# First-head silu written with exponentials, and two steps of the last head moved, in a gated recurrence

## What is computed

```python
q, f, i, g = jnp.split(h @ w_in, 4, axis=-1)
forget = lb + (1.0 - lb) * jax.nn.sigmoid(f)
key_in = 1.0 - forget
log_f = jnp.log(forget)
o = _chunk_gated_recurrence(heads(jax.nn.silu(q)), heads(key_in), heads(i), heads(log_f))
o = _rmsnorm(o, out_norm) * jax.nn.silu(heads(g))
return o.reshape(B, S, D_MODEL) @ w_out
```

## Time and profile before

| | |
|---|---|
| median of 3 runs | 2028.6 us (2027.17 to 2029.3) |
| profiled execution | 2026.63 us |
| its span in the trace | 2024.8 us |
| PE busy | 1992.9 us, 98% |
| DVE, ACT, POOL busy | 47%, 46%, 42% |
| chain that ended last | PE 93%, DVE 4%, ACT 2% |
| recurrence in the trace | about 810 to 1080 us |

### The profile page before, as it was taken

How to read it: one execution, slowest core, us unless ns; L and a number is a source line. 1 busy time by engine, 2 the same in 40 slices (tenths; PEclk the granted TensorE clock), 3 DMA queues, 4 the chain that set the end, 5 groups by cost and what they waited for, 6 DMA issues and landing times.

```text
span 2024.8 us, 26338 instructions
## 1 busy us (share of the span) xinstructions
PE 1992.9 (98%) x10823; PEld 1613.2 (80%) x10823; DVE 953.5 (47%) x1470; ACT 927.1 (46%) x1290; POOL 859.0 (42%) x672
## 2 busy tenths in 40 slices
PE   8999999999999999899999999999999999999999
PEld 7788888878888887677777888888877678888887
DVE  6644443264302316888984553255145545522551
ACT  6666563343313325666564543244366545432441
POOL 2344334526444453343334545444441254444443
PEclk9999999999999999999999999999999999999999
DMA  6122222223322321121112232222210222232321
GB/s 258 52 94 74 73 73 94 100 67 105 103 94 94 104 94 58 69 74 64 64 64 94 94 104 95 94 101 97 78 49 25 79 94 94 94 104 86 102 99 68
DMA packets 51816, 178.30 MB, mean 88 GB/s; under 512 B 5744, under 2 KB 8944, under 8 KB 51568
## 3 DMA queue, kind: packets, MB, share of 16 engines
q1 hardware_dynamic: 51696, 176.61, 25.7%
HBM read 174.49 MB, written 2.10 MB: 87 GB/s over the span
## 4 chain that ended last, share of the span: by engine, by line
PE 93%; DVE 4%; ACT 2%; issue 1%; POOL 1%; DMA 0%; SPq 0%; DVEq 0%; ACTq 0%; POOLq 0%
PE ps_gemm L228 24%; PE ps_gemm L230 24%; PE ps_gemm L229 24%; PE ps_attend L228 4%; PE ps_attend L230 4%; PE ps_attend L229 4%; PE ps_attend L1738 1%; PE ps_attend L890 1%; PE ps_attend L2522 1%; PE ps_attend L2588 1%; PE ps_attend L2523 1%; PE ps_attend L285 1%; PE ps_gemm L1718 0%; PE ps_attend L1767 0%; PE ps_attend L903 0%
## 5 line engine op out<-in xcount | busy, mean ns | idle before, releaser
L2789 POOL TENSOR_TENSOR weights_low<-weights_raw,weights_high 128x512 fp32r<-128x512 f32 (+1 forms) x332 | 427.7, 1288 | 1120.8 <-ACT weights_high L203 1120.6
L228 PE MATMUL ps_gemm<-normed_high,weights_high 128*128 128x512 f32 x1665 | 662.4, 398 | 5.4 <-DVE normed_low L1300 4.7
L230 PE MATMUL ps_gemm<-normed_low,weights_high 128*128 128x512 f32 x1665 | 648.2, 389 | 0.0
L229 PE MATMUL ps_gemm<-normed_high,weights_low 128*128 128x512 f32 x1665 | 647.8, 389 | 0.0
L203 ACT ACTIVATE weights_high<-weights_raw 128x1024 fp32r<-128x1024 f32 (+1 forms) x340 | 339.7, 1006 | 448.5 <-PE ps_attend L230 216.0
L2790 POOL TENSOR_TENSOR weights_low<-weights_raw,weights_high 128x512 fp32r<-128x512 f32 (+1 forms) x332 | 441.6, 1330 | 0.0
L228 PEld LDWEIGHTS ps_gemm<-normed_high,weights_high 128*128 128x128 f32 x1665 | 313.6, 188 | 77.7 <-issue 5.3
L230 PEld LDWEIGHTS ps_gemm<-normed_low,weights_high 128*128 128x128 f32 x1665 | 313.7, 188 | 65.8
L229 PEld LDWEIGHTS ps_gemm<-normed_high,weights_low 128*128 128x128 f32 x1665 | 313.9, 188 | 64.6 <-issue 3.6
L228 PE MATMUL ps_gemm<-operands_high_low,weights_high 128*128 128x512 f32 (+1 forms) x552 | 216.2, 392 | 0.9 <-POOL weights_low L2790 0.5
L230 PE MATMUL ps_gemm<-operands_high_low,weights_high 128*128 128x512 f32 (+1 forms) x552 | 214.2, 388 | 0.0
(11 more groups left out here) (322 smaller groups left out, 2097.7 us busy)
## 6 DMA issues: line engine op xcount, KB each, us to landing
weights_raw<-weights_full SPq DMA_DIRECT2D x317, 512.0 KB, 3.2
weights_raw<-weights_short SPq DMA_DIRECT2D x24, 128.0 KB, 2.0
residual<-x_tiles SPq DMA_DIRECT2D x4, 512.0 KB, 8.5
out_tiles<-residual SPq DMA_DIRECT2D x8, 256.0 KB, 2.1
parameters<-params SPq DMA_DIRECT2D x1, 1559.5 KB, 11.7
scratch<-memory_tiles SPq DMA_DIRECT2D x2, 256.0 KB, 4.7
scratch<-memory_tiles SPq DMA_DIRECT2D x1, 512.0 KB, 6.1
scratch<-positions SPq DMA_DIRECT2D x1, 256.0 KB, 11.8
```

Of the source, the lines that this page charges most:

```text
L228: t.op.matmul(out, m.wh[:, c:c + P], xh, start=start and n == 0, stop=False, skip_group_check=True)
L229: t.op.matmul(out, m.wl[:, c:c + P], xh, start=False, stop=False, skip_group_check=True)
L230: ins = t.op.matmul(out, m.wh[:, c:c + P], xl, start=False, stop=stop and n == len(pairs) - 1, skip_group_check=True)
L2789: g.op.tensor_tensor(m.wl[:, a], m.raw[:, a], m.wh[:, a].bitcast(F32), ALU.subtract)
```

## The change

Three edits, all within the recurrence.

1. The silu of head 0's queries is no longer ACT's silu with two table loads around it. `act_first_gate` makes the sigmoid of q with exp, ln and exp, before `act_log` of head 0, into the free tile `o`. DVE multiplies it in place into the queries (`first_queries`), between `dve_forget` and `dve_cum`. `queries_done` names the event for whoever waits.
2. In the last head ACT's `act_head_rstd` for head 6 moves from behind `act_decays` of level 4 to the place ahead of `high_to(m, s, u + 3)`.
3. In the last head DVE's `dve_g` (the scaled gate) moves from behind the factors of level 6 to behind `dve_keep_level` of level 6.

```diff
@@ pe_head
-    t.wait_ge(*m.A.at("hgrn", "q", i))
+    t.wait_ge(*queries_done(m, i))
@@
+def act_first_gate(m, s):
+    x = Head(m)
+    s.wait_ge(*m.V.at("hgrn", "q", 0))
+    s.op.activation(x.o, x.qs, ACT.Exp, scale=-1.0).then_inc(*m.A.mark("hgrn", "q_exp"))
+    s.wait_ge(*m.A.at("hgrn", "q_exp"))
+    s.op.activation(x.o, x.o, ACT.Ln, bias=m.col("one")).then_inc(*m.A.mark("hgrn", "q_ln"))
+    s.wait_ge(*m.A.at("hgrn", "q_ln"))
+    s.op.activation(x.o, x.o, ACT.Exp, scale=-1.0).then_inc(*m.A.mark("hgrn", "q_sigmoid"))
+
+def queries_done(m, i):
+    return m.A.at("hgrn", "q", i) if i else m.V.at("hgrn", "first_queries")
@@ act_head
     if not last:
         act_sigmoid(m, s, i + 1)
+    else:
+        act_head_rstd(m, s, i - 1)
     high_to(m, s, u + 3)
     act_decays(m, s, i, 4)
-    if i:
+    if i and not last:
         act_head_rstd(m, s, i - 1)
@@ act_recurrence
     act_sigmoid(m, s, 0)
+    act_first_gate(m, s)
     act_log(m, s, 0)
-    act_silu(m, s, "q", 0, x.qs)
-    s.tables(LOGEXP)
@@ dve_factors
-        v.wait_ge(*m.A.at("hgrn", "q", i))
+        v.wait_ge(*queries_done(m, i))
@@ dve_head
     dve_factors(m, v, i, 6)
-    dve_g(m, v, i)
     if not last:
+        dve_g(m, v, i)
         dve_distances(m, v, i + 1, 0)
     dve_keep_level(m, v, i, 5)
     if not last:
         dve_distances(m, v, i + 1, 1)
     dve_keep_level(m, v, i, 6)
+    if last:
+        dve_g(m, v, i)
@@ dve_recurrence
     dve_forget(m, v, 0)
+    x = Head(m)
+    v.wait_ge(*m.A.at("hgrn", "q_sigmoid"))
+    v.op.tensor_tensor(x.qs, x.qs, x.o, ALU.mult).then_inc(*m.V.mark("hgrn", "first_queries"))
     dve_cum(m, v, 0)
```

## The result

| | before | after |
|---|---|---|
| median of 20 runs | 2027.88 us | 2030.61 us |
| lowest to highest | 2025.04 to 2029.47 | 2029.47 to 2031.55 |
| ratio of the runs, 95% interval | | 1.0014 (1.0007 to 1.002) |
| span of the profiled execution | 2024.8 us | 2028.5 us |
| table loads from 800 to 1090 | 20 | 18 |

The changed kernel is slower by 0.14%, 2.7 us between the medians. The prediction was 2030.2 us. The change is within the 0.2% that the prediction called no change, though its interval lies clear of 1 on the slow side. The spans of the two profiled executions differ by 3.7 us, more than the medians do.

What follows compares the result with a forecast made beforehand. TensorE, busy 98% of the span, was taken as the bound, so only its idle time or clock could win. Terms -1.01 + 1.20 + 1.4 = +1.6 us on a median of 2028.6 gave 2030.2 us, range 2026.9 to 2031.7.

Steps and rivals of the forecast that it cites:

- Edit 1, -1.01 us: Head 0: without the table loads, level 1 starts 1.01 us sooner, bounds 0 and 1.27, and the gain lasts.
- One sign named as wrong: Head 0: its idle times growing by what its start wins would show the prediction wrong; no size given.
- Edit 2, the copy: Last head: unit copy behind the factor makes step 0 1.96 us late; less 0.76 spare, net loss 1.20 us, bounds 0.70 and 1.58.
- the pair: Last head: POOL's two subtractions of the third unit, ahead of step 0, take 3.08 us, bounds 2.56 and 3.46.
- The clock of the last head: Last head: a new TensorE idle of 2.45 us may bring 1.2 GHz, costing 0 to 1.7 us, taken as 1.4.
- The clock of head 0: Head 0's end: idle times stay as long, so both stretches at 1.2 GHz were left as they were.
- Rival C: As B, but the 1 us shift lets head 0 keep 2.4 GHz at its end: -1.7 us, 2027.1 us, chance 0.13.
- Edit 3: Last head: scaled gate moved later; ACT's silu ends later but 1.3 us of cover remain, so costed at nothing.
- Rival A: The forecast itself, all terms including the last head's clock fall: 2030.2 us, chance 0.40.
- B: The forecast without a fall of the clock in the last head: +0.2 us, 2028.8 us, chance 0.32.
- Rival F: Last head: late third unit idles TensorE so long that two slow stretches follow: +4.0 to +4.3 us, 2032.7 us, chance 0.03.
- Rival D: Last head: TensorE does not wait for the unit copy, both idle times go: -1.01 - 0.76, 2026.8 us, chance 0.06.

Runs made afterwards that it cites:

- e3_copy_ahead: Kernel before plus edit 2 with its two calls swapped, so the last head's unit copy precedes the former factor: 2027.47 us, ratio 0.9997.
- e9: Changed kernel with ACT's order in the last head made wait for the sum, unit copy, then former factor: 2026.8 us, ratio 0.9991 to before.
- e7: Kernel before with one added wait: the last head's unit copy waits for TensorE's sum, the factor stays late: 2028.8 us, ratio 1.0003.
- e5: Changed kernel with the last head's unit copy ahead of the former factor again, edits 1 and 3 kept: 2025.79 us, ratio 0.999 to before.
- e1_gate: Kernel before plus edit 1 alone, head 0's silu by exponentials: 2026.98 us, ratio 0.9993.
- e6: As e5, and in head 0 DVE keeps levels 5 and 6 before the gate and head 1's first distances: 2022.32 us, ratio 0.9973 to before.
- e4_late_g: Kernel before plus edit 3 alone, the last head's scaled gate behind level 6: 2027.91 us, ratio 0.9996.
- e2: Kernel before plus edit 2 alone, the former factor ahead of the unit copy in the last head: 2031.63 us, ratio 1.0015.
- e12: Changed kernel with DVE's norm step of head 6 moved behind level 4's factors in the last head: 2030.12 us, ratio 1.0009 to before.
- e10: As e6, and head 1's running sum also goes behind head 0's level 6: 2023.58 us, ratio 0.9976 to before.
- e11: As e10, and in head 0 level 5's exp precedes the silu's table load, its factors level 6's distances: 2023.29 us, ratio 0.9974 to before.

## Why the prediction was right, step by step

**Edit 1, -1.01 us: right.** Measured 0.98 us at level 1 and at L1715. L1715 came 33.89 to 33.91 us after L1903 in the five traces without edit 1, and 32.89 to 32.93 us in the six that have it and the old order at head 0's end, whatever the clock did. Where two executions had the same slow stretches, H0 differs by 0.92 us (after against e3_copy_ahead) and by 1.04 us (e9 against e7). The gate cost ACT's log 0.05 us and the running sum 0.12 us against L1903 (4.63 instead of 4.51 us), predicted 0.04 and 0.10. The table loads left no drain in either trace: 0.01 to 0.02 us lay between a load and its neighbours. One sign named as wrong did appear, an idle time of head 0 that grew (L1715's, by 1.35 us), yet the gain was there: the sign did not allow for a TensorE that reaches the wait sooner.

**Edit 2, the copy: right in place, too small in size.** L203 came 2.55 us later against L285, as predicted (2.54). POOL's start came 1.90 us later, predicted 1.85. The step that was mis-sized is the pair: 3.66 us, where 3.08 was taken and 3.46 was the upper bound, which rested on one contended POOL instruction of 1.73 us; one of 1.98 us occurred. Step 0 was thus 2.58 us late instead of 1.96. The spare was mis-sized the other way: the row's 0.76 us counts from a modelled end of the last matmul. Without a wait `pe_across` follows step 0's start by 2.13 us (e5), so the spare was 3.05 - 2.13 = 0.92 us. The copy's net is 2.58 - 0.92 = 1.66 us, predicted 1.20.

**The clock of the last head: right.** The price was put at 1.4 us. From step 0 to L1767 it took 3.20 us instead of 2.13, and from there to level 3 it took 4.02 instead of 3.59: 1.50 us together. The sum of the last head is 1.66 + 1.50 = 3.16 us, H7 says 3.10, and the prediction had 2.6.

**The clock of head 0: an open term left at zero.** The prediction said that the idle times stay as long. That held for the one ahead of level 5 (2.46 us) but not for L1715's (3.58 instead of 2.23), since at 2.4 GHz TensorE ended level 6 sooner and waited longer for the same copy. The slow stretch then fell wholly on the path: +1.3 us against e1_gate, which differs in the last head only. The traces agree on the size: from L1715 to the end of H0 it took 190.1 us in e6, which has no slow clock there, 190.8 to 191.0 us in the seven traces with one slow stretch behind the old order, and 191.9 to 192.1 us in the four with nearly 6 us of slow clock behind L1715. This does not explain why the profiled executions differ by more than the medians, 3.7 against 2.7 us: the profiled execution of the changed kernel was 0.3 us below its median, that of before 1.3 us below. The 3.7 us are 0.36 ahead of L1903, 0.28 in H0 and 3.10 in H7. Rival C, less slow clock on the path, did not come: e1_gate and e5 had one stretch on the path like before, the changed kernel two.

**Edit 3: right**, nothing in e4_late_g. In the changed kernel the silu ended at 1069.8, 1.4 us before the square started at 1071.26, predicted 1.3.

**The total.** -1.0 + 3.1 = +2.1 us with head 0's clock unchanged, against 2.7 us between the medians (1.4 to 4.1 by the interval) and +1.6 predicted. That 2030.2 us came within 0.4 us of the median is in part luck: the sum was 1.1 us too small, and the base of 2028.6 us, a median of three runs, 0.7 us too high against the 2027.88 us of twenty. Rival A, the forecast, is what happened; B needed an unbroken clock in the last head, and of the three executions with the copy behind the factor (after, e2, e12) none had it. Rival F was to decide from an idle of about 2.8 us; the idle was 3.08, 3.08 and 2.82 us in these three, and one slow stretch followed each, not two. Rival D's claim that the copy is not what TensorE waits for is refuted by e3_copy_ahead.

## What to carry to other kernels

Before an instruction is moved up in an engine's list, look at what it overtakes and ask who waits for that. Here 0.9 us of idle was real, and one of the two calls that the factor overtook fed a three-step chain (ACT, POOL, TensorE) with 0.7 us of slack; swapping two lines turned +3.1 into -1.0 us. Where TensorE idles over 2 us for one of its feeders, reorder that feeder's list so that what TensorE waits for comes first: the keeps of levels 5 and 6 stood behind 1.3 and 3.5 us of DVE's work for later (the gate and the next head's distances), and moving them won 3.5 us, the clock's part included. Shortening the idle times further, in e10 and e11, won nothing, since the wait moved to the next head.

## What the runs showed of the hardware

In the recurrence an idle time of TensorE of 2.5 us ahead of level 5 is in the traces of before, after, e1 and e6 alike; 1.2 GHz followed in before and not in the other three. Idle times of 2.8 to 3.6 us there ended in, or were followed by, 1.2 GHz in each trace that had one. Short idle times are no safeguard: in e11 none was longer than 1.78 us, and 3.4 us at 1.2 GHz followed; in e10 the longest was 1.92 us, and none did. The length of the slow part behind head 0 was 0, 3.4, 6.8 or 10.2 us for like schedules, and H0 differs by up to 1.3 us with it. So for a difference of one microsecond only executions with like slow stretches can be compared.

A subtraction of 128x512 on POOL took from 1.27 to 1.99 us in these rows. The shortest were not alone: DVE's instructions beside them took 1.41 and 1.31 us instead of 0.29 and 0.28. Beside the long ones a DVE instruction of 128x256 took up to 1.49 us instead of 0.42.
